# Prompt attention with unnormalised probabilities: the inverse sums are transposed beside them and multiply the value products as VectorE takes these out of PSUM

## The reference, cut to what matters

```python
def _attend(q, k, v, pos_q, pos_k, frame_causal, cum_q=None, cum_k=None):
    logits = jnp.einsum('bqhd,bkhd->bhqk', q, k).astype(jnp.float32) * scale
    ...
    p = jax.nn.softmax(jnp.where(mask, logits, NEG_INF), axis=-1)
    return jnp.einsum('bhqk,bkhd->bqhd', p.astype(v.dtype), v)
```

## Time and profile before

| what | value |
|---|---|
| median of 3 runs | 2833.5 us (2830.48 to 2834.81) |
| profiled execution, its own time | 2821.3 us |
| its span, first to last instruction | 2819.4 us |
| granted TensorE clock, mean | 0.990 |
| TensorE, VectorE, ScalarE, GpSimd busy over the span | 2697.5, 1742.5, 1054.5, 1049.3 us |
| prompt attention, layer 0 and layer 1 | 236 to 516 us, 1638 to 1916 us |

### The profile page before, as it was taken

The page is one execution under the profiler, slowest core; times in us unless marked ns, Lnnn a source line. Parts: engine busy times, 40 slices in busy tenths (PEclk is TensorE's granted clock), DMA queues, the critical chain, the costliest instruction groups (busy, mean ns, idle before and its releaser), DMA issues.

```text
span 2819.4 us, 39619 instructions
## 1 busy us (share of the span) xinstructions
PE 2697.5 (96%) x14966; PEld 2175.5 (77%) x14966; DVE 1742.5 (62%) x2196; ACT 1054.5 (37%) x1969; POOL 1049.3 (37%) x594
## 2 busy tenths in 40 slices
PE   8998999899999999999999989999999999999997
PEld 6985666787888887888879756667878888878886
DVE  4036777635564559888740467775365464688887
ACT  4225545423423233333332255554243233333333
POOL 1111000114545456767511210001145445567766
PEclk9999999999999999999999999999999999999999
DMA  4212001432343456343132200023423433654441
GB/s 144 64 30 61 25 17 44 136 135 98 123 156 114 151 187 242 127 141 128 62 115 66 65 22 17 17 66 114 164 76 134 153 134 130 251 178 141 134 145 74
DMA packets 164722, 308.75 MB, mean 110 GB/s; under 512 B 24720, under 2 KB 90416, under 8 KB 164592
## 3 DMA queue, kind: packets, MB, share of 16 engines
q1 hardware_dynamic: 161280, 303.59, 31.3%
q10 hardware_dynamic: 3312, 3.41, 0.4%
HBM read 207.40 MB, written 97.72 MB: 108 GB/s over the span
## 4 chain that ended last, share of the span: by engine, by line
PE 83%; DVE 9%; issue 3%; ACT 2%; DMA 2%; POOL 1%; SPq 0%; DVEq 0%; ACTq 0%
PE ps L2574 7%; PE ps L2484 7%; PE ps L2578 7%; PE ps L2576 7%; PE ps L2485 7%; PE ps L2486 7%; PE ps L2250 6%; PE ps L2100 6%; PE ps L2102 6%; PE ps L2101 6%; PE ps L2094 5%; PE ps L2301 3%; PE ps L2217 1%; PE ps L2361 1%; PE ps L2429 1%
## 5 line engine op out<-in xcount | busy, mean ns | idle before, releaser
L2574 PE MATMUL ps<-wq_hi,sa_hi 128*128 128x512 f32 x896 | 349.3, 390 | 5.3 <-DVE x L2030 5.3
L2578 PE MATMUL ps<-wq_hi,sa_lo 128*128 128x512 f32 x896 | 348.7, 389 | 0.0
L2576 PE MATMUL ps<-wq_lo,sa_hi 128*128 128x512 f32 x896 | 348.6, 389 | 0.0
L2030 DVE TENSOR_TENSOR x<-ps,x 128x1024 f32<-128x1024 f32 x224 | 264.2, 1213 | 54.8 <-PE ps L2578 50.5
L1968 DVE TENSOR_TENSOR sa_lo<-ra,sa_hi 128x1024 fp32r<-128x1024 f32 x112 | 279.3, 2495 | 23.4 <-ACT sa_hi L1471 23.4
L1082 POOL TENSOR_TENSOR wq_lo<-wsum,wq_hi 128x1024 fp32r<-128x1024 f32 x64 | 157.4, 2461 | 289.7 <-ACT wq_hi L1451 289.7
L2100 PE MATMUL ps<-w_hi,hT_hi 128*128 128x512 f32 (+2 forms) x672 | 248.4, 370 | 0.2 <-DVE hT_lo L1640 0.2
L2102 PE MATMUL ps<-w_hi,hT_lo 128*128 128x512 f32 (+2 forms) x672 | 246.2, 366 | 0.0
L2101 PE MATMUL ps<-w_lo,hT_hi 128*128 128x512 f32 (+2 forms) x672 | 245.4, 365 | 0.0
L1960 DVE TENSOR_TENSOR cq<-ps,cq 128x1024 f32<-128x1024 f32 x48 | 58.6, 1222 | 285.3 <-ACT cq L1512 243.2
L1088 POOL TENSOR_TENSOR wq_lo<-bsum,wq_hi 128x1024 fp32r<-128x1024 f32 x64 | 171.5, 2690 | 113.3 <-ACT wq_hi L1462 113.3
(11 more groups left out here) (323 smaller groups left out, 6188.7 us busy)
## 6 DMA issues: line engine op xcount, KB each, us to landing
ra<-hidden_scratch SPq DMA_DIRECT2D x112, 512.0 KB, 3.3
hidden_scratch<-cq SPq DMA_DIRECT2D x94, 512.0 KB, 2.7
rq<-in_w_up_dram SPq DMA_DIRECT2D x64, 512.0 KB, 3.9
rq<-in_w_down_dram SPq DMA_DIRECT2D x64, 512.0 KB, 4.3
residual_scratch<-x SPq DMA_DIRECT2D x27, 512.0 KB, 3.1
x<-residual_scratch SPq DMA_DIRECT2D x27, 512.0 KB, 7.9
x<-in_x_prompt_dram SPq DMA_DIRECT2D x16, 512.0 KB, 6.7
w_raw<-in_w_in_dram SPq DMA_DIRECT2D x16, 512.0 KB, 4.5
```

Of the source, the lines that this page charges most:

```text
L2574: pe.matmul(out, ah[:, k, :], bh[:, k * 512:(k + 1) * 512], start=new and k == 0, stop=False, skip_group_check=True)
L2576: pe.matmul(out, ah[:, k, :], bl[:, k * 512:(k + 1) * 512], start=False, stop=False, skip_group_check=True)
L2578: last = pe.matmul(out, al[:, k, :], bh[:, k * 512:(k + 1) * 512], start=False, stop=final and k == 1, skip_group_check=True)
```

## The change: what it does

The probabilities stay as ScalarE writes them. In place of the small reciprocal and the scaling, VectorE writes the reciprocal of each head's sum 64 times in a row into `ginv` (128x64 for each head). A pair of heads gives a 128x128 block, which TensorE transposes like a block of probabilities, behind them in the same unit. So the unit that ends a pair has one block more for each pair, and chunk numbers run on over them. The copy of that chunk puts the transposed inverses into `ptb`, where each column holds one query's inverse in 64 rows for each head. When the value products are done, VectorE multiplies them with that block and writes `omixT`, and ScalarE's copy is gone. A buffer of `ptb` is free once that multiplication is done (`o_ev`), not after the product alone (`pv_mm`). TensorE's transposes wait for the exponentials (`sm_done`), and the inverse block also for the reciprocal (`inv_ok`). No unit has more than 4 heads any more, so the unit with all 8 `mla` heads of tile 0 becomes two.

There are 92 units, 74 of them attention, 170 chunks a layer in place of 144, and 50 groups in place of 49.

```diff
 def tile_units(kind, t):
-    n = min(HEADS[kind], 1024 // head_stride(kind, t))
+    n = min(HEADS[kind], 4, 1024 // head_stride(kind, t))
...
+def inverse_blocks(u):
+
+    _, _, h0, heads = UNITS[u]
+    return heads // 2 if heads > 1 else h0 % 2
...
-        _chunks += (len(key_blocks(_u)) * UNITS[_u][3] + 3) // 4
+        _chunks += (len(key_blocks(_u)) * UNITS[_u][3] + inverse_blocks(_u) + 3) // 4
...
     blocks = [(g, b) for g in range(UNITS[u][3]) for b in key_blocks(u)]
+    blocks += [("inverse", k) for k in range(inverse_blocks(u))]
     return [(CHUNK0[u] + i, blocks[4 * i:4 * i + 4]) for i in range((len(blocks) + 3) // 4)]
...
+        ginv = at("ginv", LATT + 9216, [P, 4, 4, HD])
...
# ScalarE: the copies of the odd chunks (VectorE's of the even ones alike)
                                 if ch >= NPTB:
-                                    act.wait_ge(pv_mm.sem, pv_mm.at(l, group_of_chunk(ch - NPTB) + 1))
+                                    act.wait_ge(o_ev.sem, o_ev.at(l, group_of_chunk(ch - NPTB) + 1))
...
-                    if i >= LAG and group_ending(i - LAG) is not None:
...
-                        nc.scalar.copy(omixT[t % 2][:, c0:c0 + pairs, :].rearrange("p k n -> p (k n)"),
-                                       bank(6 + n % 2)[:, 0:pairs * P]).then_inc(o_ev.sem, 1)
...
# VectorE
-                        chain.link(nc.vector.reciprocal(inv, sums))
-                        for g in range(heads):
-                            probs = pbuf[n % 4][:, g * w:(g + 1) * w]
-                            last = nc.vector.tensor_scalar(probs, probs, inv[:, g:g + 1], None, ALU.mult)
-                        last.then_inc(norm_ok.sem, 1)
+                        nc.vector.reciprocal(ginv[:, GROUP_OF[u] % 4, g0:g0 + heads, :],
+                                             sums.unsqueeze(2).broadcast_to([P, heads, HD])).then_inc(inv_ok.sem, 1)
...
+                    if i >= LAG and group_ending(i - LAG) is not None:
...
+                        dve.wait_ge(pv_mm.sem, pv_mm.at(l, n + 1))
+                        nc.vector.tensor_tensor(omixT[t % 2][:, c0:c0 + pairs, :].rearrange("p k n -> p (k n)"),
+                                                bank(6 + n % 2)[:, 0:pairs * P],
+                                                ptb[ch % NPTB][:, i0:i0 + pairs * P],
+                                                ALU.mult).then_inc(o_ev.sem, 1)
...
# TensorE, probs_transposes(u)
-                    pe.wait_ge(norm_ok.sem, norm_ok.at(l, n + 1))
+                    pe.wait_ge(sm_done.sem, sm_done.at(l, u + 1))
...
                         for i, (g, b) in enumerate(blocks):
-                            c0 = (g * len(tiles) + b - tiles[0]) * P
-                            last = turned(bank(4 + ch % 2)[:, i * P:(i + 1) * P], pbuf_b[n % 4][:, c0:c0 + P])
+                            if g == "inverse":
+                                if b == 0:
+                                    pe.wait_ge(inv_ok.sem, inv_ok.at(l, n + 1))
+                                src = ginv_b[:, GROUP_OF[u] % 4, 2 * b:2 * b + 2, :].rearrange("p h d -> p (h d)")
+                            else:
+                                c0 = (g * len(tiles) + b - tiles[0]) * P
+                                src = pbuf_b[n % 4][:, c0:c0 + P]
+                            last = turned(bank(4 + ch % 2)[:, i * P:(i + 1) * P], src)
```

More of the change, by code:

```diff
@@ L149, in chunks_of, with inverse_place @@
     blocks = [(g, b) for g in range(UNITS[u][3]) for b in key_blocks(u)]
+    blocks += [("inverse", k) for k in range(inverse_blocks(u))]
     return [(CHUNK0[u] + i, blocks[4 * i:4 * i + 4]) for i in range((len(blocks) + 3) // 4)]
+def inverse_place(u):
+    ch, i = divmod(len(key_blocks(u)) * UNITS[u][3], 4)
+    assert i + inverse_blocks(u) <= 4
+    return CHUNK0[u] + ch, i * P
 def scores_behind(kind, t):
@@ L175 @@
 ACT_CHAIN, POOL_CHAIN = 1, 2 * NT + 1
-DVE_CHAIN = 8 + 2 * NT + (NATTN + 2 * NSWA) + (2 * NI + 4)
+DVE_CHAIN = 8 + 2 * NT + 2 * NSWA + (2 * NI + 4)
 SCALE64 = HD ** -0.5
@@ L388, in bits @@
             return at(f"{name}_bits", offset, shape, F32R)
+        ginv_b = bits("ginv", LATT + 9216, [P, 4, 4, HD])
         pbuf_b = [bits(f"pbuf{i}", RING + i * 4096 if i < 3 else NRM, [P, NPT * P]) for i in range(4)]
@@ L1748, in _ @@
                         kind, t, h0, heads = UNITS[u]
-                        n, w = ATTN[u], len(key_blocks(u)) * P
-                        sums, inv = den[:, n % 4, 0:heads], rinv[:, n % 4, 0:heads]
+                        n, g0 = ATTN[u], h0 % 2 if heads == 1 else 0
+                        sums = den[:, n % 4, 0:heads]
                         dve.wait_ge(sm_done.sem, sm_done.at(l, u + 1))
@@ L1798, in _ @@
                                                             ALU.subtract).then_inc(max_done.sem, 1)
+                    if i >= LAG and group_ending(i - LAG) is not None:
+                        n = group_ending(i - LAG)
+                        kind, t, h0, _ = UNITS[GROUPS[n][0]]
+                        pairs = sum(UNITS[u][3] for u in GROUPS[n]) // 2
+                        ch, i0 = inverse_place(i - LAG)
+                        if ch % 2:
+                            dve.wait_ge(pt_act.sem, pt_act.at(l, ch // 2 + 1))
+                        if t >= 2 and n == TILE_END[t - 1]:
+                            dve.wait_ge(mix_out[t % 2].sem, mix_out[t % 2].at(l, 16 * (t // 2)))
+                        c0 = {"fox": 0, "mla": 2, "swa": 6}[kind] + h0 // 2
+                        dve.wait_ge(pv_mm.sem, pv_mm.at(l, n + 1))
[3 more added lines that the diff above has]
+                                                ALU.mult).then_inc(o_ev.sem, 1)
                 nc.vector.tensor_copy(qpeS[0:ROPE].rearrange("p s h q -> p h s q"),
```

4 lines of the change are left out of this document (2 added, 2 removed).

## The result

The changed kernel takes 2933.4 us, median of four runs (2928.8 to 2936.2), against 2834.2 (2830.5 to 2837.4) for the kernel before: a ratio of 1.036, 95% interval 1.033 to 1.040. The forecast was 2866 with a range of 2834 to 2900, so the direction was right and the loss, 99 us, three times the 32 forecast. The profiled execution took 2936.2 us, its span 2934.3.

The account below looks back on a forecast made before the run. TensorE was taken to bound the kernel. Scaling -25, transposes +11.7, third-chunk waits +44 and loop end +1.6 made +32 us, giving 2866 us from a median of 2833.5; range 2834 to 2900.

Parts of the forecast that it names:

- What bounds the kernel, what goes: Prompt attention: TensorE sets the pace; removing the scaling gives back 25 us of its idle time, at most 38.
- What VectorE gets: VectorE's wide reciprocals and output multiplications: 218 us a layer instead of 205; 0.53 us per 64-wide reciprocal.
- I put it at nothing: Cost of VectorE's wide reciprocals to TensorE: none, as they are wanted more than a turn after they can start.
- 218 of 280: VectorE's forecast busy time against a layer's prompt attention, in us, used to argue that VectorE is not the bound.
- VectorE becomes the bound: Rival: slower wide reciprocals make maxima and copies late in every tile, 36 us more, 2900 us; chance 0.05.
- First of TensorE's terms, the transposes: 64 extra inverse transposes a layer on TensorE, 0.091 us each, all on the path: 11.7 us.
- The third chunk: Units with 9 or 10 blocks make TensorE wait for their first chunk's copy, 44 times: 44 us, bounds 26 and 60.
- For the 11 on VectorE ... I take 0.9: Mean wait in us for the 11 units a layer whose first chunk VectorE copies: 10 us a layer.
- a mean of 1.0 ... since a stall lets the copier catch up for the next unit: Mean third-chunk wait in us, lowered from 1.2, taking the total from 52 to 44 us.
- The clock falls too: Rival: TensorE's granted clock drops after 16 units' waits of 1.8 us, adding 27 us, 2893 us; chance 0.10.
- Buffers held longer, the end of the loop: Holding `ptb` until the multiplication costs nothing; query copies behind VectorE's last multiplication cost 0.8 us a layer, 1.6 in all.
- The signs: Expected profile: some 44 copy waits, 26 to 60 us; stretches some 16 us longer each; tiles 4 to 6 no slower.

Follow-up runs that it names:

- e3: The kernel before without the reciprocals and the scaling of the probabilities, so outputs are not divided by the sums: 2801.6 us, ratio 0.990.
- e5: The changed kernel with the third chunk's transposes issued behind the turn's scores and VectorE's copy of it behind the turn's reciprocal: 2855.8 us, ratio 1.010.
- the fillers: The changed kernel with unread 512-column matmuls on TensorE ahead of each third chunk's wait: three took 2929.7 us (ratio 1.035), one 2908.0 (1.028).
- e13: The changed kernel with third-chunk transposes behind the turn's scores, and narrow reciprocals with a copy that spreads them: 2837.6 us, ratio 1.002.
- e10: The changed kernel with inverse blocks in the values' bank, transposed behind the group's value products, and narrow reciprocals with a spreading copy: 2814.7 us, ratio 0.994.

## Why the prediction was wrong, step by step

**What bounds the kernel, what goes.** Right. The scaling was worth 28 us without its work (e3), 25 forecast.

**What VectorE gets.** All durations were right; the estimate of 8.3 ns an element was not borne out (6.3 measured). "I put it at nothing" was wrong: 19 to 23 us. The step that failed here is the comparison "218 of 280": a sum over eight tiles of 13 to 45 us. In tiles 0 and 1 VectorE is the bound or beside it. It is the rival "VectorE becomes the bound", with another mechanism (four heads of 64 columns in short turns at the forecast duration, not a slower reciprocal) and some 20 us in place of 36.

**First of TensorE's terms, the transposes.** 6.5 us with an interval of 1 to 11, 11.7 forecast: "all on the path" was too much.

**The third chunk: the step that failed.** The mechanism and the count of 22 a layer, 11 on each copier, were right; the size was not. The sum has 44 us for it. The profile has 67.5 us of such waits, above my bound of 60, and hiding them gives back 75 us, the clock included (e5). Two steps of the working failed. "For the 11 on VectorE ... I take 0.9" was 1.62: ahead of its copy stand the maxima of the turn before (1.82 us in tile 3), and in tile 1 a wide reciprocal as well. The 16 us a layer for the 11 on ScalarE came out right in total (31.8 in both), though not in its parts: the query unit that I had put near the floor of 0.53 waits 1.42 in tile 3, behind a copy of queries. And "a mean of 1.0 ... since a stall lets the copier catch up for the next unit" took 8 us off the 52 of the count; the timeline of tile 3 shows a stall after which nothing was caught up.

**"The clock falls too", chance 0.10.** It was no rival but a part of the likeliest case, and at some 45 us larger than the 27 that it was given. "The engine stays busier than it was there" was a guess from one pair of rows; the same case had shown that the lower level follows idle time. The Trainium skill (TensorE: Matmul & The Clock Gate, What's actually happening) has the low level as the default that activity releases; the fillers agree, with the clock of layer 0's stretch at 0.93, 0.97 and 0.99 for none, one and three (layer 1: 0.90, 0.97, 0.97).

**Buffers held longer, the end of the loop.** The first stream scores of layer 0 start 2.4 us after the last value products end (563.4 to 565.8), 1.5 before (516.0 to 517.6): the forecast 0.8 a layer is 0.9. VectorE's copy of `qlat` ends at 565.65, just ahead of them. That `ptb` held until the multiplication "costs nothing" is not tested alone.

**The signs.** The waits of the third chunks came 44 times, as foretold, but made 67.5 us, not 26 to 60. The stretches grew by 47 and 55 us, not 16. The tiles with few third chunks were said to be no slower; of the eight stretches between copies of the queries the fifth to seventh went from 39.7, 41.3 and 45.0 to 42.6, 45.5 and 47.9 us. Each has its `swa` unit with a third chunk, which I had counted, and then set against a gain that was only 1.2 to 1.7 us (38.0, 39.6 and 43.8 in e3_no_scaling).

**The sum again.** Scaling -28, transposes +6.5, wide reciprocals +20, third chunks with the clock that follows them +75: +74 of the 103 that the ratio gives. The rest, some 29 us with about 16 to either side, most of it from the interval of e3, is in e13, which has neither price and is yet 7 us over the kernel before, where -28 + 6.5 would put it 22 under. e10 is 24 us faster than e13. It differs in that the inverse has no chunk at all: no third chunks to copy, `ptb` not held, its transposes a turn later. VectorE's load is not the reason, for it is busy for 193.5 us of layer 0's stretch in e10 and 179.5 in e13; TensorE's clock there is 1.00 and 0.98. Which of the differences counts stays open.

## What to carry to other kernels

When a change adds one block to a unit that just filled its double buffer, price the wait by all that the copier has to do between the scores and its copy, and let no stall be caught up, since that work starts from what the stall has held up; then look whether the same work can stand one place later, which was worth 75 us here. Put a fall of the clock into the likeliest case, not into a rival, wherever the change adds idle time to the engine that it governs. And compare an engine's busy time with the bound's tile by tile: a sum over long and short turns hides the short ones.

## What the runs showed of the hardware

- VectorE's reciprocal takes 6.3 ns a column over 64 to 256 columns ((1750 - 544) / 192), six times a product's 1.03. A reciprocal of one number a head and a copy that spreads it cost less than the wide one, 20 us in this kernel.
- A matmul of 512 columns in front of each wait, 43.8 us of work that nobody reads, made a kernel 24 us faster while the granted clock rose (0.97 for 0.93 in layer 0).
- At the lower level a stretch looks as busy as it can be (4.00 of 4.00 at 0.50): of the 102 us lost, the rows of idle time show only half.
